# Top-256 key selection of the two widest query tiles: threshold bits from sign sums in place of rounds of eight, with a fourth score buffer

## What is computed

```
sc = indexer_scores(qiblk, wblk, ki)                    # 4 small heads, relu, weighted sum
sc = where(key_chunk <= q_chunk, sc, -inf)              # chunks of 64 frames
_, idx = lax.top_k(sc, 256)                             # the sample: top 80 of 320
o = selected_attention(qblk, gather_rows(k, idx), gather_rows(v, idx), valid)
```

## Time and profile before

| what | value |
|---|---|
| median of three runs | 2792.51 us (2787.89 to 2805.3) |
| span of the profiled execution | 2790.9 us |
| `block_c_in`, slots 18 to 35 | about 1310 to 1408 us |
| `block_c_mixer`, keys turned | 1408 to 1439 us |
| `block_c_mixer`, places 0 to 8 | 1439 to 1874 us |

### The profile page before, as it was taken

The page is one execution under the profiler, slowest core; times in us unless marked ns, Lnnn a source line. Parts: engine busy times, 40 slices in busy tenths (PEclk is TensorE's granted clock), DMA queues, the critical chain, the costliest instruction groups (busy, mean ns, idle before and its releaser), DMA issues. The chain is left out here.

```text
span 2790.9 us, 36346 instructions
## 1 busy us (share of the span) xinstructions
PE 2646.1 (95%) x14198; PEld 2323.7 (83%) x14198; DVE 1546.9 (55%) x2793; ACT 922.8 (33%) x1762; POOL 175.6 (6%) x168
## 2 busy tenths in 40 slices
PE   7999999999999999979969988899999999999996
PEld 6778789989899999868757777887898999999895
DVE  2445363444444444566889799963634444444535
ACT  3207343323222222322044555562532222223231
POOL 0300040000000000300020000000400000000003
PEclk9999999999999999989965898899999999999998
DMA  4110311101010101131100000003110101011011
GB/s 136 46 41 1 115 49 45 61 30 60 30 60 30 60 30 45 61 94 31 44 8 1 1 1 1 1 30 121 59 46 31 60 30 59 31 42 48 30 46 65
DMA packets 81279, 124.25 MB, mean 45 GB/s; under 512 B 6224, under 2 KB 54736, under 8 KB 81168
## 3 DMA queue, kind: packets, MB, share of 16 engines
q1 hardware_dynamic: 81168, 122.74, 13.4%
HBM read 110.98 MB, written 11.75 MB: 44 GB/s over the span
## 5 line engine op out<-in xcount | busy, mean ns | idle before, releaser
L1213 PE MATMUL psum<-xt_hi,layer_w_hi 128*128 128x384 f32 (+1 forms) x1536 | 505.5, 329 | 3.2 <-DVE xt_lo L847 3.2
L1215 PE MATMUL psum<-xt_hi,layer_w_lo 128*128 128x384 f32 (+1 forms) x1536 | 505.0, 329 | 0.0
L1214 PE MATMUL psum<-xt_lo,layer_w_hi 128*128 128x384 f32 (+1 forms) x1536 | 504.9, 329 | 0.0
L1128 DVE TENSOR_TENSOR act<-psum,act 128x512 f32<-128x512 f32 x540 | 366.2, 689 | 233.6 <-PE psum L1251 230.7
L1249 PE MATMUL psum<-layer_w_hi,layer_h_split 128*128 128x512 f32 x1024 | 400.0, 391 | 2.8 <-DVE layer_h_split L1116 1.6
L1250 PE MATMUL psum<-layer_w_lo,layer_h_split 128*128 128x512 f32 x1024 | 399.3, 390 | 0.0
L1251 PE MATMUL psum<-layer_w_hi,layer_h_split 128*128 128x512 f32 x1024 | 399.1, 390 | 0.0
L1116 DVE TENSOR_TENSOR layer_h_split<-layer_h_raw,layer_h_split 128x384 fp32r<-128x384 f32 (+1 forms) x192 | 98.4, 512 | 352.8 <-ACT layer_h_split L1029 352.8
L1213 PEld LDWEIGHTS psum<-xt_hi,layer_w_hi 128*128 128x128 f32 x1536 | 288.3, 188 | 4.7 <-DVE xt_lo L847 3.5
L1214 PEld LDWEIGHTS psum<-xt_lo,layer_w_hi 128*128 128x128 f32 x1536 | 288.4, 188 | 1.3
L1215 PEld LDWEIGHTS psum<-xt_hi,layer_w_lo 128*128 128x128 f32 x1536 | 288.4, 188 | 0.0
(11 more groups left out here) (215 smaller groups left out, 4067.5 us busy)
## 6 DMA issues: line engine op xcount, KB each, us to landing
layer_w_raw<-in_ff_w SPq DMA_DIRECT2D x64, 1024.0 KB, 6.3
ab_in_w_raw<-in_ab_w_in SPq DMA_DIRECT2D x12, 512.0 KB, 4.5
c_in_w_raw<-in_c_w_in SPq DMA_DIRECT2D x12, 512.0 KB, 3.9
ab_in_xt_raw<-in_xT SPq DMA_DIRECT2D x8, 512.0 KB, 4.2
layer_resid<-in_x SPq DMA_DIRECT2D x16, 256.0 KB, 2.8
x_scratch<-act SPq DMA_DIRECT2D x8, 512.0 KB, 2.6
layer_resid<-x_scratch SPq DMA_DIRECT2D x16, 256.0 KB, 2.7
out_y_prompt<-act SPq DMA_DIRECT2D x8, 512.0 KB, 2.6
```

The source lines that it names most:

```text
L1128: dve.tensor_tensor(acc, banks[4 + g % 4][0:r], acc, ALU.add).then_inc(y_read, 1)
L1213: pe.matmul(out, w1_hi[:, k, w], xt_hi[:, k, a:b], start=(k == 0), stop=False)
L1214: pe.matmul(out, w1_hi[:, k, w], xt_lo[:, k, a:b], start=False, stop=False)
L1215: mm = pe.matmul(out, w1_lo[:, k, w], xt_hi[:, k, a:b], start=False, stop=(k == KT - 1))
```

## The change

- `RING` is 4: m = 3 has a buffer of its own and needn't wait for m = 0's. The three ranks scored in `block_c_in` are now called `SCORED_EARLY`.
- Ranks 1 and 2 have no rounds. ACT counts by a sum of signs how many scores of a row lie above a threshold, and DVE sets one bit of the threshold's 32-bit pattern by that count. 32 steps for each of the two ranks, two a slot: m = 1 in slots 17 to 32, m = 2 in slots 18 to 33. The signs are written to PSUM banks that nobody reads.
- At the start of `block_c_mixer` DVE settles the threshold's last bit (`settle`) and makes the mask, ties included (`mask`), in place of the ten rounds.
- Ranks 3 to 6 begin one place earlier (m = 3 at x = 4), and their rounds lie by a new list.
- The two rounds of m = 0 in slots 18 and 19 stay. A semaphore `barred` tells ACT that the future keys are masked.

```
-RING = 3
+RING = 4
+SCORED_EARLY = 3
+BISECTED = [1, 2]
+STEPS = 32
...
+class Bisect:
+    def signs(self, act, i, k, junk):
+        m = BISECTED[i]
+        bias = 0.0 if k == 0 else self.bits[:, i:i + 1].bitcast(F32)
+        if k >= 1:
+            act.wait_ge(self.moved[i], k)
+        act.activation(junk[:, 0:nkeys(C_RANKED[m])], self.scored(m), ACT.Sign, bias=bias, scale=-1.0,
+                       accum_out=self.sums[:, i:i + 1]).then_inc(self.summed[i], 1)
+    def move(self, dve, i, k):
+        above = nkeys(C_RANKED[BISECTED[i]]) - 2 * TOPK
+        bits, flip, bit = self.bits[:, i:i + 1], self.flip[:, i:i + 1], STEPS - 1 - k
+        dve.wait_ge(self.summed[i], k + 1)
+        dve.tensor_scalar(flip, self.sums[:, i:i + 1], float(above), -1.0 if k == 0 else float(2 ** bit),
+                          ALU.is_gt, ALU.mult).then_inc(self.flips_made[i], 1)
+        dve.wait_ge(self.flips_made[i], k + 1)
...
+            ins = dve.scalar_tensor_tensor(out=bits, in0=flip, scalar=1 << (bit - 1), in1=bits,
+                                           op0=ALU.bitwise_xor, op1=ALU.bitwise_xor)
...
+        ins.then_inc(self.moved[i], 1)
...
+class Cut:
+    def settle(self, dve, junk):
+        for i, m in enumerate(BISECTED):
+            nk = nkeys(C_RANKED[m])
+            ins = dve.tensor_scalar(junk[:, i, 0:nk], self.scored(m), self.bits[:, i:i + 1].bitcast(F32), None,
+                                    ALU.is_gt, ALU.add, accum_out=self.over[:, i:i + 1])
+        self.link(dve, ins)
... (seven more links on [P, n] columns)
+    def mask(self, dve, i, equal, counted):
...
+        self.link(dve, dve.tensor_scalar(ct, scored, cut, None, ALU.is_gt, ALU.add, accum_out=self.over[:, i:i + 1]))
+        self.link(dve, dve.tensor_scalar(left, self.over[:, i:i + 1], -1.0, float(TOPK), ALU.mult, ALU.add))
+        self.link(dve, dve.tensor_scalar(eq, scored, cut, None, ALU.is_equal))
+        self.link(dve, dve.tensor_tensor_scan(ct, eq, eq, 0.0, ALU.add, ALU.max))
+        self.link(dve, dve.scalar_tensor_tensor(out=eq, in0=ct, scalar=left, in1=eq, op0=ALU.is_gt, op1=ALU.mult))
+        self.link(dve, dve.scalar_tensor_tensor(out=ct, in0=scored, scalar=cut, in1=eq, op0=ALU.is_lt, op1=ALU.max))
+        dve.tensor_scalar(scored, ct, MASKED, None, ALU.mult).then_inc(self.masked, 1)
...
 block_c_in
+        for i, (slot, a_slot) in enumerate([(2 * NT - 1, 2), (2 * NT, 2)]):
+            for k in range(STEPS):
+                steps_at.setdefault(slot + k // a_slot, []).append((k % a_slot, i, k))
...
 ScalarE
+            act.wait_ge(ranking.relu_done, SCORED_EARLY * IDX_HEADS)
+            signs(2 * NT - 1)
             for j in range(2, len(chunks)):
-                for n in st.next_pieces(j):
-                    st.split_hi(act, n)
+                for t in range(NT):
+                    if t == NT - 1:
+                        for n in st.next_pieces(j):
+                            st.split_hi(act, n)
+                    signs(j * NT + t)
...
 VectorE, after the splits and ahead of the slot's wait for its product
+                    moves = sorted(steps_at.get(g, []))
+                    for half, i, k in moves:
+                        if half == 0 and j >= 2:
+                            bisect.move(dve, i, k)
                     dve.wait_ge(done, g + 1)
...
 VectorE, after the slot's rope
-                        x = t + ROUND_TILES * (j - 2)
-                        if t < ROUND_TILES:
-                            ranking.take(dve, [0, 1] if x < rounds(0) - 8 else [1])
+                    elif g in (2 * NT, 2 * NT + 1):
+                        ranking.take(dve, [0])
+                    for half, i, k in moves:
+                        if half == 1 or j == 1:
+                            bisect.move(dve, i, k)
...
 block_c_mixer
+    begin = {m: 4 if m == SCORED_EARLY else HP * (m - 1) for m in range(SCORED_EARLY, NR)}
...
-            items_at[HP * m + x_item].append((m, i))
-            mixes_at[HP * m + x_mix].append((m, i))
+            items_at[begin[m] + x_item].append((m, i))
+            mixes_at[begin[m] + x_mix].append((m, i))
...
-    early_2 = rounds(2) - 2
-    spread(1, rounds(1) - ROUNDS_BEFORE - ROUNDS_AHEAD, 0, RING * HP)
-    spread(2, early_2 - ROUNDS_AHEAD, 0, RING * HP)
-    spread(2, rounds(2) - early_2, RING * HP, (RING + 1) * HP)
-    for m in range(RING, NR):
-        spread(m, rounds(m) // 2, HP * m + 5, HP * (m + 1))
-        spread(m, rounds(m) // 2, HP * (m + 1), HP * (m + 2))
+    for m, parts in {3: [(14, 9, 48), (10, 48, 64), (8, 64, 80)], 4: [(5, 53, 64), (12, 64, 80), (15, 80, 96)],
+                     5: [(4, 69, 80), (11, 80, 96), (17, 96, 112)], 6: [(2, 85, 96), (10, 96, 112), (20, 112, 128)]}.items():
+        for count, lo, hi in parts:
+            spread(m, count, lo, hi)
...
 ScalarE: q_idx_high(3) after q_high(0), idx_queries(3) after queries(0, 3); GpSimd: q_idx_low(3) after q_low(0)
-            for _ in range(ROUNDS_AHEAD):
-                ranking.take(dve, [1, 2])
+            cuts.settle(dve, counts)
+            for i in range(len(BISECTED)):
+                cuts.mask(dve, i, counts[:, 0], counts[:, 1])
```

More of the change, by code:

```diff
@@ L173, in encoder @@
         xt_lo = split.take("xt_lo", [P, KT, TOK], F32R)
-        top_at = (nc.sbuf_usable_end - 4 * (sum(IDX_WIDTH) + 8 * RING)) // 32 * 32
+        top_at = (nc.sbuf_usable_end - 4 * (sum(IDX_WIDTH) + 8 * RING + 2 * 8)) // 32 * 32
         top = Room(nc, "c_", top_at)
-        rank0_at = top_at + 4 * (IDX_WIDTH[0] - nkeys(C_RANKED[0]))
-        idx = [top.take(f"idx_scores{n}", [P, w]) for n, w in enumerate(IDX_WIDTH)]
+        rank0_at = top_at + 4 * (IDX_WIDTH[RING - 1] + IDX_WIDTH[0] - nkeys(C_RANKED[0]))
+        idx = {n: top.take(f"idx_scores{n}", [P, IDX_WIDTH[n]]) for n in [RING - 1, *range(RING - 1)]}
         top8 = top.take("top8", [P, RING, 8])
+        bits = top.take("threshold_bits", [P, len(BISECTED)], I32)
         w1_at = (split.end - 2 * 4 * KT * FC) // 32 * 32
@@ L1377, in mix, with prompts @@
             if t < SAMPLE:
-                self.step(m, dve.memset(out[0:CHUNK, nk - CHUNK:nk], BARRED))
+                dve.memset(out[0:CHUNK, nk - CHUNK:nk], BARRED).then_inc(self.barred, 1)
+    def prompts(self, m):
+        return sum(t < SAMPLE for t in C_RANKED[self.first:m + 1])
     def eight(self, m):
@@ L1415, in product, with __init__ @@
         mm.then_inc(self.i_done, 1)
+class Bisect:
+    def __init__(self, nc, c, tag, room, scored, bits):
+        self.scored, self.bits = scored, bits
+        n = len(BISECTED)
+        self.sums = room.take("sign_sums", [P, n])
+        self.flip = room.take("bits_to_flip", [P, n], I32)
+        sem = lambda what: [c(nc.semaphore(tag + f"{what}{m}")) for m in BISECTED]
+        self.summed, self.flips_made, self.moved = sem("signs_summed"), sem("flips_made"), sem("threshold_moved")
+    def signs(self, act, i, k, junk):
[12 more added lines that the diff above has]
+        dve.wait_ge(self.flips_made[i], k + 1)
+        if k == 0:
+            ins = dve.tensor_scalar(bits, flip, 1 << (bit - 1), None, ALU.bitwise_xor)
+        elif bit > 0:
+            ins = dve.scalar_tensor_tensor(out=bits, in0=flip, scalar=1 << (bit - 1), in1=bits,
+                                           op0=ALU.bitwise_xor, op1=ALU.bitwise_xor)
+        else:
+            ins = dve.tensor_tensor(bits, flip, bits, ALU.bitwise_xor)
+        ins.then_inc(self.moved[i], 1)
@@ L1503, in _ @@
                 pool.sem_clear(sem_range)
-            for m in range(RING):
+            for m in range(SCORED_EARLY):
                 r = rows(C_RANKED[m])
@@ L1653, in _, with block_c_mixer @@
                         beside(t)
[L1656 removed]
+def block_c_mixer(nc, room, A, kc, vc, ki, qi, wi, idx, top8, bits, ident, ident_r, next_early, ps):
     tag = "c_mix_"
@@ L1730, in block_c_mixer @@
         qS = sb("q_stacked", [P, 2, HP, P], F32R)
+        counts = Room(nc, tag, room.at - 4 * HP * P).take("cut_counts", [P, 2, SEQ])
         qi_tok = sb("q_idx_split", [P, 2, IDX_HEADS, 2, HD], F32R)
@@ L1736, in block_c_mixer @@
         rden = sb("rden", [P, 2, HP])
-        rel = sb("relu", [P, 2, SEQ])
+        rel = sb("relu", [P, 2, max(nkeys(t) for t in RANKED[SCORED_EARLY:])])
         prep = room.from_here(tag)
@@ L1840, in queries @@
                 r = rows(ORDER[p])
+                if p == 1 and g == 0:
+                    act.wait_ge(cuts.masked, len(BISECTED))
                 if p >= 2 and g == 0:
@@ L1969, in _ @@
                     outputs(p, 0)
-                if h == HP - 1 and 2 <= p < NT - 1:
+                if h == HP - 1 and SCORED_EARLY <= p - 1 and p < NT - 1:
                     ranking.close(dve, p - 1)
```

105 lines of the change are left out of this document (73 added, 32 removed).

## The result

The changed kernel takes 2756.9 us (median of four runs, 2753.9 to 2757.5) against 2792.9 for the kernel before; the ratio is 0.986, 95% interval 0.983 to 0.989. That is 36 us less, where 55 were forecast: faster by over 1%, inside the range, and 19 us slower than the forecast. The span went from 2790.9 to 2752.2 us.

The account below looks back on a forecast made before the run. VectorE's rounds were taken to bound the mixer, with TensorE at half clock in places 0 to 2 and TensorE bounding the query chunks; 13 + 2 - 8 - 10 - 19 - 33 = -55 gives 2738 us, range 2708 to 2770.

Parts of the forecast that it names:

- places 0 to 2: Mixer places 0 to 2: VectorE's rounds and a TensorE at 1.2 GHz are two close limits; forecast -8, -10 and -19 us.
- The clock's return within place 1: Without VectorE cutting in between heads, TensorE's full clock returns within place 1; places 1 and 2 take 24.5 and 25 us.
- the rival: Places 0 to 2: the clock stays at half speed throughout, total -31 us, 2761 us; chance 0.24.
- Query chunks, +13: Slots 17 to 26: slots of 5.15 us make VectorE 11.2 us late, plus 2 for a clock fall; bounds +3 and +22.
- No slack: Query chunks, splits of slot 26: TensorE already stood still there, so VectorE's 11.2 us of lateness all go on the path.
- nothing of 1024 columns on ScalarE takes over 1.154: Argument against the rival of signs too long in the query chunks (2825 us, chance 0.06).
- Start of the mixer, +2: Start of the mixer: two more ScalarE copies and one more GpSimd subtraction ahead of its key splits cost 2 us.
- It stays covered: Start of the mixer: settle and mask, 20 us together, fit in some 24 us covered; at 30, 6 us would show.
- Places 3 to 8, -33: Mixer places 3 to 8: fewer or moved rounds save 36 us, less 3 kept for clock falls.
- microsecond or two: Places 3 to 8: each place takes the later of VectorE's and TensorE's sums plus this allowance.
- VectorE's sums: VectorE's predicted work at places 3 to 7: 51.7, 59.7, 57.9, 46.3 and 32.5 us.
- TensorE's terms: TensorE's predicted need at full clock, 0.43 us per head and 128 keys: 60 at place 3, then 52, 45, 37, 29.

## Why the prediction was right, and where it was off

- **What bounds which place.** Right: places 0 to 2 were VectorE's rounds and a TensorE at half speed. The clock's return within place 1, the step that I had doubted most (0.24 for the rival), came 4 us into it (a mean of 0.90 over its 20 us), and the kernel before without its rounds shows the cause. Places 0 to 2 gave 37 us, as forecast, but that the sum fits is luck: place 0 gave 2.3 us too little, place 1, where the clock came early, 4.5 too much, place 2 2.2 too little.
- **Query chunks, +13, measured +9.2.** The mechanism is the one described; the slot is 4.94 us rather than 5.15, so VectorE is 9.4 us late rather than 11.2. "No slack" was wrong: those 9.4 us reach TensorE as gaps of 7.6 us where it had 0.97, only 6.6 more. The other 2.6 go with the clock's fall at that place, for which I had 2: the first twelve matmuls behind the gap follow at 0.43 us, those before it at 0.23. One reading of the prediction is wrong, without weight for the sum: "nothing of 1024 columns on ScalarE takes over 1.154" overlooks the layer norm's pass of 128x1024, 1.243 us (L344); the sign took 1.109.
- **Start of the mixer, +2, measured +6.6: the cost of the masks, which I set at nothing.** The +2 was for the added copies and the subtraction, and without the masks 1.6 remain. "It stays covered" looked at the time in which VectorE waits, and VectorE indeed waited 3.35 us after the masks. What I left out is that GpSimd's splits run beside it: the masks slowed them, and TensorE waits for them. The ten rounds that stood there before had left the splits at 1.28 us, so the rows of before gave no price. The Trainium skill has the rule, on the page "SBUF — State Buffer", section "SBUF: two separate sides": VectorE and GpSimd share a pair of ports, which one of them holds for a whole instruction, and on VectorE's side instructions with two SBUF inputs or in a 2-port mode want it. The trace agrees: scan and weighted adds wait (3.24 and 2.10 us for 2.28 and 1.28 alone), the count doesn't (1.28 and 1.28). That the first heads came at 1454, as forecast, is luck again: the query chunks were 3.8 us cheaper and this stage 4.6 dearer.
- **Places 3 to 8, -33, measured -16.8: the main miss.** The step that failed is the "microsecond or two" on top of the later of the two sums: at places 4 and 5 it was 7.4 and 5.1 us on VectorE's busy time. VectorE's sums were right (59.7 predicted, 59.09 busy at place 4; 57.9 and 57.20 at place 5; 46.3 and 46.15 at place 6). TensorE's terms were 5 to 7 us below the floor of places 4 to 6; that doesn't make TensorE the later of the two, but it leaves hardly any slack at place 4. And the list of rounds, which I read only for its counts, has heads with three rounds beside heads with none. With the same counts laid evenly and in pairs of different ranks, and a clock of 1.00, places 4 and 5 take 118.5 us against the 119.6 predicted. At place 6 it was the clock: 56.4 us at a mean of 0.85, 49.8 at 1.00 with the same list. I had kept 3 us for such falls, and this one alone took 6.6.

What stays open: why the clock falls in place 6 in some kernels with that list of rounds and not in others, and how much of the gain at places 4 and 5 is due to the even spread and the mixed pairs and how much is the clock's.

## What to carry to other kernels

When two engines are near their limits in the same stretch, count on the later of the two sums only if the filler work is laid evenly over the steps and the clock holds; a pair of independent small jobs at a step is cheaper than two that depend on each other. Before calling a piece of VectorE's work covered, look at what GpSimd does beside it, and whether the new instructions are of the kind that hold GpSimd up. A stall on TensorE costs more than its length where the clock falls behind it (a gap of 3.40 us here, while behind one of 3.00 in another kernel it held): look at the granted clock of the stretch that follows.

## What the runs showed of the hardware

- A scan of 1024 fp32 columns takes 2.28 us (2.02 at 896), nearly twice a weighted add (1.28); beside GpSimd's splits 3.24.
- A GpSimd subtraction of 128x512 takes 1.28 us alone and up to 3.16 beside VectorE's masks, while beside MAX8 and MATCH_REPLACE8 it kept its 1.28 in the kernel before.
- A sign of 1024 columns that is written to PSUM takes 1.109 us (993 ns at 896 columns), and loads no table.
- The same 16 heads with the same list of rounds took 49.8 us at a mean clock of 1.00 and 56.4 at 0.85.
- After a MATCH_REPLACE8 of 640 keys (0.81 us) an instruction that needs its result starts 0.85 us after it, an independent one 0.72.
